# Decay exponents of a state-space mixer from DMA-broadcast rows and a minimum, in place of bfloat16 products on TensorE

## The chip, the cores and the metric

The kernel runs on one core of a Trainium2 chip. The metric is the device time of one execution in microseconds, as the median of several runs; one more execution was profiled. "ScalarE", "VectorE", "GpSimd" and "TensorE" stand as ACT, DVE, POOL and PE in the profile; PEld is TensorE's loading of weights, SP the engine that issues most loads.

## The reference

One layer of a trunk on 128 context tokens and 512 latent tokens, in five tiles of 128 tokens (`NJ` = 5): an input projection, a convolution, a Mamba-2 mixer with 16 heads in both directions beside a pooling mixer, an output projection and a mixture of 16 experts. The change concerns the part of the mixer inside one chunk of 128 tokens:

```python
A_cum = jnp.cumsum(A, axis=-1)                      # A = dt * a, per head
scores = jnp.einsum("bclhn,bcshn->bhcls", Cc, Bc) * jnp.exp(segsum(A))
y_diag = jnp.einsum("bhcls,bcshp->bclhp", scores, xd)   # xd = x * dt
...
y_f, s_f = ssd_direction(..., dt_bias[0], a_log[0], ..., reverse=False)
y_b, s_b = ssd_direction(..., dt_bias[1], a_log[1], ..., reverse=True)
y = (y_f + y_b).reshape(b, L, D_SSD)
y = rmsnorm(y * jax.nn.silu(z.astype(F32)), ssd_norm_w)
```

`exp(segsum(A))` is, for a source token s and a target token t, the exponential of the difference of two cumulative sums, below the diagonal for the forward direction and above it for the backward one.

## The kernel before

Each engine has its program written out by hand in one block; the engines wait for each other by semaphores, and each executes its own program strictly in order. The program runs through these stages: loads and the first norm, the feature projection in 20 tiles (f = 0 to 19, TensorE, L503), the convolution, the products of B and C (`gT`), the pooling products, the chunk states, then the **decay stage**, the output projection (L711), the router and the experts (L815, L827).

The decay stage goes through 40 steps i, two heads of one token tile in each; `j = i // 8` is the token tile. Four steps are a group, numbered g here (`jg` in the code): half the heads of a tile. In step i:

- TensorE, `exponents(i)` (L647 to L665): seven bfloat16 products build the exponents of both heads and both directions in one bank, 512 columns: one with a mask of large negative numbers (L652), two that subtract the cumulative sum of the source token (L656), four that add that of the target token (L662). The sums stand as three bfloat16 pieces each in `tabT`, made by VectorE in L1320 to L1337 from ten products on TensorE (L586).
- ScalarE, `exps(i)` (L958): the exponential, from the bank to a buffer `wbuf`.
- GpSimd (L1167): times dt.
- VectorE, `decay_scores(i)` (L1371, L1374): times `gT`, and forward plus backward.
- TensorE, `diagonal(i)` (L677): the two heads' products with x, from `wbuf`.

Around it stands the gate z of each group, z(g): `project_z(g)`, eight products over k (L575) in one bank, spread over the first three steps of the group before as three, three and two k; ScalarE's `tanh_z(g)` (L951) and VectorE's `silu_z(g)` (L1379), which on their engines stand ahead of the fourth step's work; and the outputs of a group: `from_states` (TensorE, L687, first step, from the second token tile on), `begin_outputs` (VectorE, L1388 to L1396, fourth step, five operations from the second token tile on, one before), `end_outputs` (L1406, L1408, third step of the next group), `turn_y` (TensorE, L697) and `copy_y` (VectorE, L1417). In the last four steps parts of the output projection stand in place of z. On TensorE the diagonal runs three steps behind the exponents:

```python
            for i in range(NS + 3):
                if i < NS:
                    exponents(i)
                    if i % 4 < 3 and i // 4 + 1 < 2 * NJ:
                        project_z(i // 4 + 1, (range(0, 3), range(3, 6), range(6, 8))[i % 4])
...
                if i >= 3:
                    k = i - 3
                    diagonal(k)
```

Of the kernel before, what the change touches and what calls it, by code (L numbers as in the profile page):

```python
# [29 lines left out]
P = 128  # L30
D = 1024
# [19 lines left out]
WBUFS = 6  # L51
# [10 lines left out]
B_STRICT, B_MASK, B_STACK, B_ALL = 0, 128, 384, 416  # L62
# [23 lines left out]
def trunk_kernel(nc, consts, bconsts, vecs, rows, inv, fnorm, x, states0, w_ring, w_late, b_late, w_dt,  # L86
                 w_pool, w_router, w_exp, y_out, s_out):
    ctx = ExitStack()
    with ctx:
# [3 lines left out]
        def sem(name):  # L93
# [5 lines left out]
        slot_out = nc.dram_tensor("slot_out", [SLOTS - P, D], F32).ap()  # L99

# [18 lines left out]
        idb = sb("idb", [P, P], BF16)  # L119
        maskb = sb("maskb", [P, 2, P], BF16)  # L120
        strictb = sb("strictb", [P, P], BF16)
        onesb = sb("onesb", [P, P], BF16)
        stackb = sb("stackb", [96, 32], BF16)
        nstackb = sb("nstackb", [96, 32], BF16)
# [42 lines left out]
        bcst = uf[:, 2 * D:2 * D + B_ALL]  # L167
        tabT = [bf_[0:96, d * 320:(d + 1) * 320].bitcast(BF16) for d in range(2)]
        yt = [bf_[:, 640:1152], ex[:, 11776:12288]]

        wbufs = [ex[:, 8192 + i * 512:8192 + (i + 1) * 512].rearrange("p (h d t) -> p h d t", h=2, d=2)
                 for i in range(WBUFS)]
        sout = [zf[:, 2048 + d * D:2048 + (d + 1) * D] for d in range(2)]
        split_r = [ex[0:32, 8192 + i * TOK:8192 + (i + 1) * TOK] for i in range(2)]
        mid = zf[0:32, 4096:4416].bitcast(BF16)
# [7 lines left out]
        MASK4 = maskb[:, :, :].unsqueeze(1).to_broadcast([P, 2, 2, P])  # L183

        def wbuf(i):
            return wbufs[i % WBUFS]

# [14 lines left out]
        s_bconst = sem("bfloat16_constants_loaded")  # L202
# [52 lines left out]
        s_tabs = sem("decay_tables_split")  # L255
# [7 lines left out]
        s_wd = sem("decays_times_dt")  # L263
        s_e = sem("exponents_built")
        s_ex = sem("decays_exponentiated")
        s_w = sem("scores_decayed")
# [90 lines left out]
        def _(sp):  # L357
# [18 lines left out]
            sp.dma_start(bcst, bconsts).then_inc(s_bconst, 16)  # L376
# [26 lines left out]
            for j in range(NJ):  # L403
                if j == NJ - 1:
# [4 lines left out]
                    sp.wait_ge(s_ex, NJ * HG)  # L409
# [30 lines left out]
        def _(pe):  # L440
# [21 lines left out]
            def ada_late(q):  # L462

                if q == 0:
                    pe.wait_ge(s_dif, 1)
                if q >= 2:
                    pe.wait_ge(s_adr, q - 1)
# [57 lines left out]
            for f in range(20):  # L525
# [25 lines left out]
                if f == 2:  # L551
# [13 lines left out]
            def project_z(jg, ks):  # L565
# [6 lines left out]
                if ks[0] == 0 and jg >= 1:  # L572
                    pe.wait_ge(s_zs, jg)
# [73 lines left out]
            def exponents(i):  # L647
                j, hh = i // HG, 2 * (i % HG)
                o = psb[4 + i % 2]
                if i >= 2:  # L650
                    pe.wait_ge(s_ex, i - 1)
# [1106 lines left out]
```

## Time and profile before

| | |
|---|---|
| median of 3 runs | 1046.53 us (1046.01 to 1047.34) |
| profiled execution | 1048.91 us, span 1047.1 us |
| TensorE busy | 934.5 us, 89% of the span |
| VectorE, GpSimd, ScalarE busy | 360.0, 217.9, 168.9 us |
| decay stage | about 299 to 448 us |
| busy in 380 to 400 us | TensorE 19.60, VectorE 18.59, GpSimd 6.12, ScalarE 4.80 us |
| chain that ended last | TensorE 60%, VectorE 10% |

The profile's busy time of TensorE counts the modelled length of pipelined products, so how long one piece of its work holds up the next is read from start to start in the timeline, not from durations. TensorE's clock is given as the granted share of 2.4 GHz, 1.00 or 0.50.

### The profile page before, as it was taken

Reading aid. Unit: us, or ns where it says so; the run is one execution under the profiler, and the core shown is the slowest. Engines: PE = TensorE matmul, PEld = TensorE weight load, DVE = VectorE, ACT = ScalarE, POOL = GpSimd, SP = SyncE. Lnnn points to the kernel's source line nnn. Section 1 sums busy time; section 2 is a strip of 40 time slices with the busy share of each in tenths; the row PEclk is TensorE's granted clock in tenths of the full one; section 3 lists DMA queues with packets and bytes.
Section 4 is the critical chain, followed back from the end, with each engine's and each line's share of the span. In section 5 each row is a group of like instructions: output and inputs, shape, how many; then the busy total and the mean of one; then the engine's idle time right before and its main releaser. Section 6 shows DMA issues by size and latency. Waiting matters only on the chain.

```text
span 1047.1 us, 13807 instructions
## 1 busy us (share of the span) xinstructions
PE 934.5 (89%) x5470; PEld 631.0 (60%) x5470; DVE 360.0 (34%) x620; ACT 168.9 (16%) x350; POOL 217.9 (21%) x256
## 2 busy tenths in 40 slices
PE   2899999998999999999999449999999999999910
PEld 2565655555545555544444348887888877888800
DVE  2330016446755998733225431110111111111128
ACT  5111012112322222200001200010101111000123
POOL 0189996001422333200000000000000000000053
PEclk9989999999999999999999659999999999999965
DMA  8914657323100002840000418989999999999552
GB/s 356 416 81 161 243 216 285 123 81 121 41 1 1 1 1 81 356 189 20 21 20 21 160 41 305 340 327 333 330 326 351 331 327 333 320 347 326 193 215 106
DMA packets 34451, 205.32 MB, mean 196 GB/s; under 512 B 3760, under 2 KB 6384, under 8 KB 16496
## 3 DMA queue, kind: packets, MB, share of 16 engines
q1 hardware_dynamic: 22896, 169.08, 43.7%
q0 software_dynamic: 5472, 20.45, 5.2%
q10 hardware_dynamic: 6048, 15.30, 3.7%
q8 instruction: 24, 0.39, 0.1%
q14 instruction: 11, 0.09, 0.0%
HBM read 184.86 MB, written 19.96 MB: 196 GB/s over the span
## 4 chain that ended last, share of the span: by engine, by line
PE 60%; DVE 10%; issue 2%; DMA 1%; POOL 1%; ACT 1%; ACTq 0%; POOLq 0%; DVEq 0%
PE bank L815 23%; PE bank L711 13%; PE bank L827 11%; PE bank L575 6%; PE bank L800 2%; DVE ex L1355 1%; PE bank L613 1%; DVE xs L1408 1%; DVE ex L1632 1%; PE bank L764 1%; POOL ex L1167 1%; DVE ex L1371 1%; PE bank L677 1%; DVE uT L1649 1%; DMA ex<-slot_out,ri 1%
## 5 line engine op out<-in xcount | busy, mean ns | idle before, releaser
L815 PEld LDWEIGHTS bank<-yT,ex 128*128 128x128 f32 x2176 | 247.0, 193 | 9.0 <-issue 9.0
L815 PE MATMUL bank<-yT,ex 128*128 128x128 f32 x2176 | 247.2, 276 | 1.0 <-DVE yT L1610 1.0
L503 PE MATMUL bank<-hT,ring 128*128 128x512 f32 (+1 forms) x640 | 179.9, 440 | 2.4 <-DMA ring<-w_ring 2.4
L503 PEld LDWEIGHTS bank<-hT,ring 128*128 128x128 f32 x640 | 96.6, 194 | 73.7 <-issue 70.8
L827 PE MATMUL bank<-ex,yT 128*128 128x512 f32 x272 | 120.9, 597 | 0.0
L1617 DVE TENSOR_TENSOR yT<-yT,bank 128x128 f32<-128x128 f32 x68 | 19.6, 288 | 222.8 <-ACT yT L1029 222.8
L827 PEld LDWEIGHTS bank<-ex,yT 128*128 128x128 f32 x272 | 50.3, 190 | 57.8 <-issue 56.9
L575 PE MATMUL bank<-ring,hT 128*128 128x512 f32 x160 | 76.8, 615 | 4.5 <-DVE ex L1379 2.2
L1176 POOL DMA_INDIRECT yT<-h_dram,idx x17 | 17.3, 1017 | 261.7 <-PE bank L800 261.7
L711 PE MATMUL bank<-ring,yT 128*128 128x512 f32 x160 | 70.2, 593 | 0.8 <-DVE yT L1417 0.8
L1167 POOL TENSOR_TENSOR ex<-ex,dts 128x512 f32<-128x512 f32 x40 | 44.3, 1106 | 101.5 <-ACT ex L958 101.4
L1029 ACT ACTIVATE yT<-bank 128x128 f32<-128x128 f32 x68 | 18.8, 277 | 220.0 <-PE bank L815 220.0
L711 PEld LDWEIGHTS bank<-ring,yT 128*128 128x128 f32 x160 | 30.3, 190 | 38.8 <-issue 37.8
L1621 DVE COPY yT<-bank 128x512 f32<-128x512 f32 x17 | 11.8, 692 | 108.0 <-PE bank L827 108.0
L575 PEld LDWEIGHTS bank<-ring,hT 128*128 128x128 f32 x160 | 28.8, 194 | 32.5 <-issue 26.9
L1371 DVE TENSOR_TENSOR ex<-ex,gT 128x512 f32<-128x512 f32 x40 | 31.9, 797 | 25.9 <-POOL ex L1167 25.9
L1176 POOL DMA_INDIRECT yT<-h_dram,token_of x1 | 1.1, 1098 | 181.5 <-DVE token_of L1601 181.5
L958 ACT ACTIVATE ex<-bank 128x512 f32<-128x512 f32 x40 | 23.9, 597 | 85.1 <-PE bank L662 85.0
L711 PE MATMUL bank<-ring,uT 128*128 128x512 f32 x80 | 36.1, 597 | 0.0
L711 PE MATMUL bank<-hT,uT 128*128 128x512 f32 x80 | 35.3, 594 | 0.8 <-DVE bcT L1396 0.8
L1151 POOL TENSOR_TENSOR ex<-xs,dts 128x1024 f32<-128x1024 f32 x8 | 15.1, 1900 | 97.7 <-DVE xs L1296 80.1
L1308 DVE SCALAR_TENSOR_TENSOR ex<-ex,vec 128x643 f32<-128x643 f32 x36 | 33.8, 939 | 1.3
(260 smaller groups left out, 955.2 us busy)
## 6 DMA issues: line engine op xcount, KB each, us to landing
ex<-w_exp SPq DMA_DIRECT2D x102, 1024.0 KB, 6.7
ring<-w_ring SPq DMA_DIRECT2D x13, 2048.0 KB, 12.3
yT<-w_late SPq DMA_DIRECT2D x16, 1024.0 KB, 6.4
slot_out<-yT ACTq DMA_DIRECT2D x17, 512.0 KB, 8.7
slot_out<-ex POOLq DMA_DIRECT2D x9, 512.0 KB, 12.9
ex<-x SPq DMA_DIRECT2D x5, 512.0 KB, 7.7
xs<-x SPq DMA_DIRECT2D x5, 512.0 KB, 13.5
y_out<-uT SPq DMA_DIRECT2D x5, 512.0 KB, 2.6
```

Of the source, the lines that this page charges most:

```text
L503: mm = pe.matmul(o, w[:, k, (f % 4) * P:(f % 4 + 1) * P], hT[:, k, lo:hi], start=(k == 0), stop=(k == KT - 1))
L575: mm = pe.matmul(psb[6][:, :], hT[:, k, j * P:(j + 1) * P], w[:, k, :], start=(k == 0), stop=(k == KT - 1), skip_group_check=True)
L711: mm = pe.matmul(out_bank(j, hf_, c)[:, :], (yT, uT)[c][:, k, j * P:(j + 1) * P], w[:, k, :], start=(k == 0), stop=(k == KT - 1), skip_gro ...
L800: mm = pe.transpose(psb[2 + k // 4][:, (k % 4) * P:(k % 4 + 1) * P], xg[:, k * P:(k + 1) * P], ident)
L815: mm = pe.matmul(psb[c % 2][:, a * P:(a + 1) * P], w[:, a, k, :], xgT[:, k, :], start=(k == 0), stop=(k == KT - 1))
L827: mm = pe.matmul(psb[6 + hf_][:, :], aT[:, 2 * c + k, :], w[:, k, hf_ * 512:(hf_ + 1) * 512], start=(c == 0 and k == 0), stop=(c == 1 and ...
L958: act.activation(wbuf(i)[:, :, :, :], psb[4 + i % 2][:, :].rearrange("p (h d t) -> p h d t", h=2, d=2), ACT.Exp).then_inc(s_ex, 1)
L1029: act.activation(sg[c % 2], psb[c % 2][:, 0:P], ACT.Silu).then_inc(s_sg, 1)
L1167: pool.tensor_tensor(wbuf(i)[:, :, :, :], wbuf(i)[:, :, :, :], dt_h.unsqueeze(3).to_broadcast([P, 2, 2, P]), ALU.mult).then_inc(s_wd, 1)
L1308: ins = stt(cacc[f % 2], xpad[f % 2][:, q:q + 643], wq, cacc[f % 2], ALU.mult, ALU.add)
L1371: step(tt(w.rearrange("p h d t -> p (h d) t"), w.rearrange("p h d t -> p (h d) t"), gT[:, j, hh // HG, :].unsqueeze(1).to_broadcast([P, 4, ...
L1617: tt(aT[:, c, :], sg[c % 2], psb[c % 2][:, P:2 * P], ALU.mult).then_inc(s_ac, 1)
```

## The change

The cumulative sums of both directions are still made by ten products on TensorE, but early, behind the decay rates in feature tile f = 2. ScalarE copies them on chip and stores them to DRAM by four DMAs, ordered by pair of heads. In the decay stage, ScalarE's queue loads for each step one row of 512 sums (two heads, two directions, 128 target tokens), broadcast to all 128 partitions, into one of three buffers. The exponent comes from one formula for both directions, the minimum of the forward and the backward one, so no mask is needed:

- VectorE, `exponents(i)`: for each head, row of the backward sums plus a number per partition, minimum with the row of the forward sums.
- ScalarE, `exps(i)`: for each head, the exponential with a bias per partition; ahead of it the load of the row of step i + 3.
- ScalarE `mask_forward` and VectorE `mask_both`: for each head, the lower triangle times the forward dt plus the upper triangle times the backward dt, into a buffer `kbuf`.
- GpSimd, `masked_scores(i)`: `kbuf` times `gT`; then `wbuf` times `kbuf`.
- TensorE: `exponents` is gone; `diagonal(i)` stands in step i. z alternates between two banks, so that z(g+1) no longer waits for silu_z(g).

`wbuf` has four buffers of 256 columns in place of six of 512. The bfloat16 constants and their load go.

```diff
@@ project_features, f == 2 (TensorE)
+                    for j in range(NJ):
+                        for d, tri in ((0, trif), (1, trib)):
+                            o = psb[1][64:96, d * P:(d + 1) * P] if j == 0 else \
+                                psb[1][32 * d:32 * d + 32, (j - 1) * P:j * P]
+                            mm = pe.matmul(o, a_[:, j * 32:(j + 1) * 32], tri, start=True, stop=True)
+                    mm.then_inc(s_tab, 1)
@@ project_z
-                if ks[0] == 0 and jg >= 1:
-                    pe.wait_ge(s_zs, jg)
+                if ks[0] == 0 and jg >= 2:
+                    pe.wait_ge(s_zs, jg - 1)
@@ decay stage, TensorE
-            for i in range(NS + 3):
-                if i < NS:
-                    exponents(i)
-                    if i % 4 < 3 and i // 4 + 1 < 2 * NJ:
-                        project_z(i // 4 + 1, (range(0, 3), range(3, 6), range(6, 8))[i % 4])
...
-                if i >= 3:
-                    k = i - 3
-                    diagonal(k)
...
+            for i in range(NS):
+                if i % 4 < 3 and i // 4 + 1 < 2 * NJ:
+                    project_z(i // 4 + 1, (range(0, 3), range(3, 6), range(6, 8))[i % 4])
...
+                diagonal(i)
+                if i % 4 == 0 and i >= 8:
+                    from_states(i // 4)
+                if i % 4 == 1 and i >= 4:
+                    turn_y(i // 4 - 1)
@@ feature tile f == 3, ScalarE
+                    act.wait_ge(s_tab, 1)
+                    act.activation(tabr[0:64, :], psb[1][0:64, :], ACT.Copy)
+                    act.activation(tabr[64:96, 0:256], psb[1][64:96, 0:256], ACT.Copy).then_inc(s_tabc, 1)
...
@@ decay stage, ScalarE
+            def mask_forward(i):
+                j, hh = pair(i)
+                if i >= WBUFS:
+                    act.wait_ge(s_w, i - WBUFS + 1)
+                for q in range(2):
+                    c = j * 32 + hh + q
+                    ins = act.activation(kbuf(i)[:, q, :], trif, ACT.Copy, scale=dt_[:, c:c + 1])
+                ins.then_inc(s_k1, 1)
...
+                act.wait_ge(s_min, i + 1)
+                if i + RBUFS < NJ * HG:
+                    load_rows(i + RBUFS)
+                for q in range(2):
+                    c = j * 32 + hh + q
+                    ins = act.activation(wbuf(i)[:, q, :], wbuf(i)[:, q, :], ACT.Exp, bias=ncum[:, c:c + 1])
+                ins.then_inc(s_ex, 1)
...
                 exps(i)
+                if i + 2 < NJ * HG:
+                    mask_forward(i + 2)
@@ decay stage, GpSimd
+            masked_scores(0)
             for i in range(NJ * HG):
...
+                if i + 1 < NJ * HG:
+                    masked_scores(i + 1)
+                pool.wait_ge(s_kg, i + 1)
                 pool.wait_ge(s_ex, i + 1)
...
+                pool.tensor_tensor(wbuf(i), wbuf(i), kbuf(i), ALU.mult).then_inc(s_w, 1)
@@ decay stage, VectorE
+                dve.wait_ge(s_r[i % RBUFS], 16 * (i // RBUFS + 1))
+                if i >= WBUFS:
+                    dve.wait_ge(s_dg, i - WBUFS + 1)
+                r = rbufs[i % RBUFS]
+                for q in range(2):
+                    ins = stt(wbuf(i)[:, q, :], r[:, q, 1, :], fms[:, j, hh + q:hh + q + 1], r[:, q, 0, :],
+                              ALU.add, ALU.min)
+                ins.then_inc(s_min, 1)
...
                 if i % 4 == 3 and i // 4 + 1 < 2 * NJ:
                     silu_z(i // 4 + 1)
-                decay_scores(i)
+                exponents(i)
+                if i + 1 < NJ * HG:
+                    mask_both(i + 1)
```

On TensorE the order in the second half of one group (z of the next group, then the first step of that group) was, in the kernel before (L575 is z, L677 the diagonal, L652 to L662 the exponents, L687 from_states):

```order
L575 MATMUL bank6<-ring,hT 128x512 x2
L677 MATMUL bank0<-xs,ex 128x64 x2
L652 MATMUL bank5<-maskb,idb 128x512
L656 MATMUL bank5<-nstackb,bcT 128x2x128 x2
L662 MATMUL bank5<-bcT,stackb 128x128 x4
L677 MATMUL bank1<-xs,ex 128x64 x2
L652 MATMUL bank4<-maskb,idb 128x512
L656 MATMUL bank4<-nstackb,bcT 128x2x128 x2
L662 MATMUL bank4<-bcT,stackb 128x128 x4
L575 MATMUL bank6<-ring,hT 128x512 x3
```

In the changed kernel the same place reads as follows (L591 is z, L664 the diagonal, L674 from_states, L684 turn_y):

```order
L591 MATMUL bank4<-ring,hT 128x512 x2
L664 MATMUL bank0<-xs,ex 128x64 x4
L591 MATMUL bank6<-ring,hT 128x512 x3
L664 MATMUL bank1<-xs,ex 128x64 x2
L674 MATMUL bank2<-ex,bcT 128x512
L674 MATMUL bank3<-ex,bcT 128x512
L591 MATMUL bank6<-ring,hT 128x512 x3
L664 MATMUL bank1<-xs,ex 128x64 x2
L684 MATMUL bank7<-cst,xs 128x128 x4
L591 MATMUL bank6<-ring,hT 128x512 x2
```

The diagonals of the third and the fourth step, four products, now stand together directly behind the last two k of z, and the fourth is no longer two exponents and more away from it.

On VectorE the fourth step of a group now reads as follows (L1393 is silu_z, L1386 exponents, L1374 mask_both, L1402 to L1410 begin_outputs); the names in brackets are the semaphores waited for:

```order
L1393 SCALAR_TENSOR_TENSOR btok<-btok,bank6 128x512 [waits tanh_of_half_z,ssd_outputs_combined]
L1386 SCALAR_TENSOR_TENSOR ex<-bcT,dts 128x128 [waits diagonal_products,decay_rows_2_loaded]
L1386 SCALAR_TENSOR_TENSOR ex<-bcT,dts 128x128
L1374 SCALAR_TENSOR_TENSOR ex<-cst,dts,ex 128x128 [waits forward_dt_masked]
L1374 SCALAR_TENSOR_TENSOR ex<-cst,dts,ex 128x128
L1402 TENSOR_TENSOR bcT<-xs,dsum 128x512
L1408 TENSOR_TENSOR ex<-bank2,dts 128x512 [waits state_outputs,dve_steps]
L1410 TENSOR_TENSOR bcT<-bcT,ex 128x512 [waits dve_steps]
L1408 TENSOR_TENSOR ex<-bank3,dts 128x512 [waits dve_steps]
L1410 TENSOR_TENSOR bcT<-bcT,ex 128x512 [waits dve_steps]
L1386 SCALAR_TENSOR_TENSOR ex<-ex,dts 128x128 [waits diagonal_products,decay_rows_0_loaded]
```

Where decay_scores (L1371, L1374 of the kernel before) stood between silu_z and begin_outputs, the start of the step's chain stands now.

## Rows read from the trace of the kernel before

**Rows 1.** Timeline of TensorE, one group: start us, us, engine, line, operation, tiles, count.

```profile
340.29 2.84 PE L575 MATMUL bank<-ring,hT 128*128 128x512 f32 x6 [0.20 <-DVE btok L1379]
342.97 0.55 PE L677 MATMUL bank<-xs,ex 128*128 128x64 f32 x4
343.36 0.61 PE L697 MATMUL bank<-cst,xs 128*128 128x128 f32 x4
343.81 0.38 PE L652 MATMUL bank<-maskb,idb 128*128 128x512 bf16 x1
...
344.47 2.79 PE L575 MATMUL bank<-ring,hT 128*128 128x512 f32 x6
...
351.42 1.94 PE L687 MATMUL bank<-ex,bcT 128*128 128x512 f32 x4
353.19 0.38 PE L652 MATMUL bank<-maskb,idb 128*128 128x512 bf16 x1
...
354.21 1.13 PE L575 MATMUL bank<-ring,hT 128*128 128x512 f32 x2 [0.20 <-DVE btok L1379]
```

**Rows 2.** Timeline of TensorE at the start and the end of the decay stage.

```profile
299.18 0.38 PE L652 MATMUL bank<-maskb,idb 128*128 128x512 bf16 x1
...
447.62 3.70 PE L711 MATMUL bank<-ring,yT 128*128 128x512 f32 x8 [0.78 <-DVE yT L1417]
```

**Rows 3.** Timeline of ScalarE and VectorE behind z(0), whose last product was issued before 299.18.

```profile
299.38 0.60 ACT L951 ACTIVATE btok<-bank 128x512 f32<-128x512 f32 x1 [10.15 <-PE bank L575]
299.99 1.28 ACT L958 ACT_TABLE_LOAD   x1
...
300.08 0.69 DVE L1379 SCALAR_TENSOR_TENSOR btok<-btok,bank 128x512 f32<-128x512 f32 x1 [5.35 <-ACT btok L951]
```

**Rows 4.** Timeline of VectorE, two copies without a wait between them.

```profile
249.78 0.28 DVE L1295 COPY xs<-bank 128x128 f32<-128x128 f32 x1
249.99 0.68 DVE L1296 COPY xs<-bank 128x512 f32<-128x512 f32 x1
```

**Rows 5.** Groups by line and form: count, busy us, mean ns, idle before.

```profile
L1543 DVE SCALAR_TENSOR_TENSOR bcT<-bank,stat,bcT 128x512 f32<-128x512 f32 x10 | 7.5, 751 | 0.4
L1119 POOL TENSOR_TENSOR ex<-ex 128x256 f32<-128x256 f32 x2 | 1.5, 731 | 0.2
```

**Rows 6.** Timeline of ScalarE: two operations without a wait, and a DMA issue.

```profile
262.15 0.37 ACT L929 ACTIVATE uT<-bank,vec 128x128 f32<-128x128 f32 x1 [5.52 <-PE bank L613]
262.42 0.68 ACT L930 ACTIVATE uT<-bank,vec 128x512 f32<-128x512 f32 x1
...
646.85 0.36 ACTq L1035 DMA_DIRECT2D slot_out<-yT  x1
```

**Rows 7.** Timeline of GpSimd and VectorE in one group.

```profile
340.80 1.05 POOL L1167 TENSOR_TENSOR ex<-ex,dts 128x512 f32<-128x512 f32 x1 [1.83 <-ACT ex L958]
340.88 1.25 DVE L1374 TENSOR_TENSOR ex<-ex 128x256 f32<-128x256 f32 x1
342.05 0.68 DVE L1388 TENSOR_TENSOR bcT<-xs,dsum 128x512 f32<-128x512 f32 x1
...
344.94 0.69 DVE L1396 TENSOR_TENSOR bcT<-bcT,ex 128x512 f32<-128x512 f32 x1
...
348.18 0.42 DVE L1374 TENSOR_TENSOR ex<-ex 128x256 f32<-128x256 f32 x1
```

**Rows 8.** Timeline of TensorE: three k of z behind a wait.

```profile
324.75 4.46 PE L575 MATMUL bank<-ring,hT 128*128 128x512 f32 x6 [1.97 <-DVE ex L1379]
```

**Rows 9.** Windows: length, busy PE, PEld, DVE, ACT, POOL, granted clock, DMA share, GB/s.

```profile
326.00:328.00 2.00, 2.00 (x3) 0.78 (x3) 1.52 (x3) 0.00 (x0) 0.00 (x0) 0.50 0.00 0
```

**Rows 10.** Timeline of TensorE: the products of the sums.

```profile
246.66 2.37 PE L586 MATMUL bank<-cst,dts 128*32 128x128 f32 x20
```

**Rows 11.** DMA issues: count, KB each, median us from issue to landing.

```profile
ex<-states ACTq DMA_DIRECT2D x2, 512.0 KB, 4.0
xs<-x SPq DMA_DIRECT2D x5, 512.0 KB, 13.5
```

More of the change, by code:

```diff
@@ L182, in trunk_kernel, with pair, kbuf, z_bank @@
         zero_f = ex[:, 3900:3900 + D]
[L183 removed]
+        def pair(i):
+            return i // HG, 2 * (i % HG)
         def wbuf(i):
             return wbufs[i % WBUFS]
+        def kbuf(i):
+            return kbufs[i % WBUFS]
+        def z_bank(jg):
+            return psb[6 - 2 * (jg % 2)]
         def out_bank(j, hf_, c):
@@ L254, in trunk_kernel @@
         s_tab = sem("decay_tables_summed")
-        s_tabs = sem("decay_tables_split")
+        s_tabc = sem("decay_tables_on_chip")
+        s_tabst = sem("decay_tables_stored")
+        s_fms = sem("forward_less_backward_sums_ready")
+        s_r = [sem(f"decay_rows_{i}_loaded") for i in range(RBUFS)]
         s_g = sem("bc_products")
@@ L581, in _ @@
             pe.wait_ge(s_pad, CONVF)
-            for d, tri in ((0, trif), (1, trib)):
-                q = 2 + 2 * d
-                for j in range(NJ):
-                    o = psb[q + 1][0:32, 0:P] if j == 0 else psb[q][0:32, (j - 1) * P:j * P]
-                    mm = pe.matmul(o, a_[:, j * 32:(j + 1) * 32], tri, start=True, stop=True)
-                mm.then_inc(s_tab, 1)
             for j in range(NJ):
@@ L930, in scale_pooled, with load_rows @@
                 act.activation(uT[:, i, CTX:TOK], lat_in, ACT.Copy, scale=scale).then_inc(s_u, 1)
+            def load_rows(i):
+                j, hh = pair(i)
+                act.dma_start(rbufs[i % RBUFS].rearrange("p h d t -> p (h d t)"),
+                              sums_dram[j, hh // 2].rearrange("h d t -> (h d t)").unsqueeze(0).to_broadcast([P, 4 * P])).then_inc(
+                    s_r[i % RBUFS], 16)
+            for i in range(RBUFS):
+                load_rows(i)
             for i in range(4):
@@ L966, in square_y @@
                                accum_out=stat[:, 16 + jg:17 + jg]).then_inc(s_ys, 1)
+            for i in range(2):
+                mask_forward(i)
             tanh_z(0)
@@ L1418, in copy_y @@
                    vec[:, V_SN + k:V_SN + k + 4].unsqueeze(2).to_broadcast([P, 4, P]), ALU.mult).then_inc(s_yT, 1)
+            mask_both(0)
             silu_z(0)
@@ L1729, in layout @@
     return {
-        "consts": cst, "bconsts": bc, "vecs": vec, "rows": row, "inv": inv,
+        "consts": cst, "vecs": vec, "rows": row, "inv": inv,
         "w_late": w_late, "b_late": b_late.reshape(P, (NQ + 2) * P),
```

163 lines of the change are left out of this document (60 added, 103 removed).

## Prediction

> **What bounds the kernel now.** I read the chain that ended last first. Between 299 and 448 us, the stage that the change rewrites, it runs over TensorE's z products (L575) again and again, with short pieces of GpSimd, VectorE and ScalarE between. The timeline of TensorE for one group of four steps shows why [rows 1]: the group starts at 340.29 and the next at 354.21, so it takes 13.92 us, and the only waits are the two of 0.20 us at the starts. From start to start, three k of z take 2.68 us, a diagonal pair 0.39, turn_y 0.45, one step's exponents 0.66, from_states 1.77; two k of z are as long as from_states. TensorE is the bound here, and the next stages wait for it. So whatever leaves TensorE counts, if nothing else puts a wait in its place. The stage lasts from 299.18, where the last product of z(0) has been issued, to 447.62, where the output projection starts to run without a break [rows 2]: 148.4 us.
>
> **What the change removes.** 40 steps of exponents on TensorE, 40 x 0.66 = 26.4 us. The splitting of the sums on VectorE (L1320 to L1337) lies beside TensorE's pooling products and is done when they are: nothing. VectorE's two products for each step (512 and 256 wide) go, and four 128-wide operations come; ScalarE's 512-wide exponential becomes four 128-wide operations and a DMA issue; GpSimd's one 512-wide product becomes two 256-wide. None of these sums up to the length of a group, so totals don't decide. The order does.
>
> **What the change moves.** In the kernel before, diagonal(i) stands three steps behind exponents(i) on TensorE. In the changed kernel it stands in step i itself, behind the z products of that step. Take group g, and let T be the moment when TensorE has issued the last product of z(g), in step 4g-2. Ahead of it TensorE then has diagonal(4g-2) and directly diagonal(4g-1). But the exponents of step 4g-1 stand on VectorE behind silu_z(g), which waits for tanh_z(g), which waits for z(g). So between T and diagonal(4g-1) lies a chain through four engines, covered by 0.39 us of TensorE's work. The same chain was there before, but with three steps of other products on TensorE under it.
>
> **The chain, from T.** Tanh starts 0.20 after TensorE has gone on, takes 0.60, and silu starts 0.10 later [rows 3]: 0.90. Silu takes 0.69; an operation that waits for nothing starts some 0.08 before the end of the one ahead (a 128-wide copy of 0.28 is followed after 0.21 [rows 4]): exponents begin at 1.51. A VectorE operation with a scalar from a column is some 0.06 longer (751 ns [rows 5] against silu's 0.69), so a pair of 128-wide ones takes 0.27 + 0.34 = 0.61: 2.12. The trace has no such operation in this shape; bounds are 0.49 (no addition) and 0.8. ScalarE then issues the row load (0.36 [rows 6]) and computes two exponentials (0.27 + 0.37 [rows 6]): with hops of 0.03, 3.15. GpSimd has masked_scores(4g) ahead of the product: a 256-wide product with two real streams takes 0.73 [rows 5], and I take that; half of the 512-wide one with a broadcast [rows 7], 0.53, is the bound below. Could masked_scores start when mask_both(4g) is done (2.65), the product would end at 4.14. But the two engines exclude each other: the 256-wide VectorE sum took 0.42 alone and 1.25 when GpSimd's 1.05 us product had started 0.08 earlier [rows 7]. VectorE's begin_outputs starts at 2.55 with a product of 0.68 on two on-chip inputs and holds GpSimd to 3.23. So masked_scores ends at 3.96, the product at 4.70, and TensorE goes on at **4.72**, after 4.3 us of idleness.
>
> **The second chain.** VectorE's begin_outputs has five operations, 0.72 apart [rows 7]. The third meets the product on GpSimd and ends at 5.25, the fifth at 6.69. Only then come exponents(4g) (to 7.22), ScalarE (to 8.25) and GpSimd, with masked_scores(4g+1) ahead (to 9.27): diagonal(4g) can start at **9.30**. TensorE's own way there: 4.72 + 0.39 + 2.68 = 7.8, so it would wait another 1.5 us. After an idleness of 1.97 us, though, three k of z took 4.46 us [rows 8], with the granted clock at 0.50, that is 1.2 of 2.4 GHz, in 326 to 328 [rows 9]. That is 1.6 to 1.8 us more; with 1.6 TensorE is ready at 9.4. The Trainium skill (TensorE: Matmul & The Clock Gate, HAM oscillation) describes loops like this, in which TensorE waits once in every tile and starts each tile at the low clock. By that rule every group pays; the trace agrees in the one place where it has such a gap. Without the loss of clock a full group costs 0.1 us less, since the second chain then sets the end, and only the first two intervals lose the whole.
>
> **The sum.** A full group is 9.40 + 0.39 (diagonal 4g) + 1.77 (from_states) + 2.68 + 0.39 + 0.45 (turn_y) + 1.77 (two k) = **16.85 us** against 13.92. There are seven (T of z(2) to T of z(9)): 118.0. The first interval has a table load of 1.28 [rows 3] in its chain, so that diagonal(0) starts at 5.2: with 0.39 + 2.68 + 1.6 + 0.39 + 1.77, 12.0. The second has no from_states and a begin_outputs of one operation, so no second chain: 4.72 + 0.39 + 2.68 + 1.6 + 0.39 + 2.68 + 0.39 + 0.45 + 1.77 = 15.1. Behind the last T come 9.30, from_states 1.77, four diagonals (1.6), three parts of the projection at 1.77, turn_y 0.45, the eight remaining k (7.1), turn_y and copy_y (1.2): 26.7. Together 171.8 against 148.4: +23.4.
>
> The 10 products of the sums move from 246.66, where they took 2.3 us [rows 10] while TensorE would have waited for VectorE's conversions anyway (copies to 250.67 [rows 4]), to tile f = 2, where TensorE goes from tile to tile and everything behind waits for it. So +2.3; nothing is the bound below. ScalarE's copies and four DMA issues there lie in the time in which it waits for TensorE's next tile: nothing, and 3 us if that cover were gone. The constants' load that is dropped starts nothing earlier that TensorE waits for: nothing.
>
> The sum is +25.7 us. On the profiled execution's own 1048.9 us that makes 1074.6; the median of the runs shown is 1046.5, 2.4 us lower, and the prediction is made for a median: **1072 us**, a ratio of 1.025.
>
> **Row loads.** Each brings 256 KB and is issued three steps ahead. The shortest lead is that of step 4g+2, from 2.15 to some 11 after T: 8.7 us. A 512 KB load by ScalarE's queue took 4.0 us [rows 11], and the DMA share is 0.00 where I looked inside the stage [rows 9]. Only at its end, beside the output weights, did loads need 13.5 us [rows 11]. I take nothing; the bound above is the third rival.
>
> **Rivals.** (1) *Shorter chains*: no loss to the exclusion, none of clock, GpSimd's products at 0.53 to 0.73. Then the second chain ends at 8.3 to 8.8 and a full group takes 15.7 to 16.2; with shorter first intervals (10.4 and 12.9) and the sums' move at nothing to 2.3, +10 to +16: 1056 to 1063. For it: the exclusion is seen at only a few places. (2) *The other side, faster*: VectorE gets to exponents(4g-1) early enough that TensorE never waits. This holds if the chain of 4.72 shrinks to the 0.39 that covers it, or the z products end a step earlier than I read. Then 26.4 us go and 2.3 come: 1022. Against it: each link stands in order behind the one before. An idleness of 2.7 us in each of nine groups would just take up the 24.1 us, and leave 1046. (3) *Late rows*: with 13.5 us a load, the last six to eight steps wait some 2 to 4 us each: +12 to +20 on top, 1084 to 1092. The Trainium skill (DMA: Bandwidth & Descriptors, Issuing engines are not separate DMA queues) says that loads from different engines share the same 16 DMA engines; that speaks for this rival, but by the trace it touches the end of the stage alone. (4) *More exclusion*: two 256-wide GpSimd products and four VectorE operations in each step collide more often than I count. One more collision of 0.73 in each chain gives 18.3 a group, +10: 1082.
>
> **How the numbers follow.** Forecast 0.60, rival 1 0.15, rival 2 0.08, a chain that just cancels 0.03, rival 3 0.06, rival 4 0.08. The likeliest gives 1072; its own range is 1064 to 1080. The 8-in-10 range takes in rivals 1 and 4: 1055 to 1083. A measurement of this kernel tells some 0.2% from no change. Faster 0.08, same 0.03, slower 0.89.
>
> **What would show it.** In the profile after: TensorE idle for about 4 us once in each group, ended by GpSimd's product with diagonal as the waiter; the first z products behind it at the low clock; a group of about 16.9 us; TensorE's busy share of the stage near 70%; VectorE's exponents starting right behind silu and behind begin_outputs. No idle time ended by a row load. The feature stage some 2.3 us later at its end. If TensorE's groups take 11 us (7.1 of z, 1.6, 0.45, 1.77), I am wrong in the order; if they take 14 to 16, in the prices of the chain.

## The result and the profile after

The changed kernel takes 1077.3 us (median of 4 runs, 1073.5 to 1081.0) where the kernel before takes 1046.9 (4 runs, 1046.0 to 1047.7): a ratio of 1.029, 95% interval 1.0245 to 1.0335. It is slower by 30 us; forecast were 1072 us in a range of 1055 to 1083. The profiled execution took 1079.9 us, with a span of 1078.0 us and a mean granted clock of 0.928.

The rows that answer to [rows 1] are one group of four steps on TensorE in the changed kernel (start us, us, engine, line, operation, tiles, count, idle time before and its releaser). T, the moment when the last product of z is issued, is 380.85; the next T is 398.28.

```profile
380.85 0.55 PE L664 MATMUL bank<-xs,ex 128*128 128x64 f32 x4
385.41 1.11 PE L664 MATMUL bank<-xs,ex 128*128 128x64 f32 x4 [4.01 <-POOL ex L1189]
386.32 4.84 PE L591 MATMUL bank<-ring,hT 128*128 128x512 f32 x6
390.99 0.55 PE L664 MATMUL bank<-xs,ex 128*128 128x64 f32 x4
391.38 1.94 PE L674 MATMUL bank<-ex,bcT 128*128 128x512 f32 x4
393.16 2.74 PE L591 MATMUL bank<-ring,hT 128*128 128x512 f32 x6
...
398.28 0.33 PE L664 MATMUL bank<-xs,ex 128*128 128x64 f32 x2
```

TensorE issues diagonal(4g-2) at T and then stands idle for 4.01 us, until GpSimd's product (L1189) releases diagonal(4g-1). The group has lost all of the exponents (the bfloat16 products of [rows 1] are gone) and is still 17.43 us long, where [rows 1] shows 13.92. The other three engines in the same group, first VectorE:

```profile
381.75 0.69 DVE L1393 SCALAR_TENSOR_TENSOR ex<-ex,bank 128x512 f32<-128x512 f32 x1 [4.45 <-ACT ex L954]
382.36 0.61 DVE L1386 SCALAR_TENSOR_TENSOR ex<-ex,dts 128x128 f32<-128x128 f32 x2
382.88 0.61 DVE L1374 SCALAR_TENSOR_TENSOR ex<-cst,dts,ex 128x128 f32<-128x128 f32 x2
383.40 0.69 DVE L1402 TENSOR_TENSOR bcT<-xs,dsum 128x512 f32<-128x512 f32 x1
...
387.28 0.61 DVE L1386 SCALAR_TENSOR_TENSOR ex<-bcT,dts 128x128 f32<-128x128 f32 x2
```

and GpSimd:

```profile
383.57 1.11 POOL L1180 TENSOR_TENSOR ex<-ex,gT 128x256 f32<-128x256 f32 x1 [5.69 <-DVE ex L1374]
384.64 0.72 POOL L1189 TENSOR_TENSOR ex<-ex 128x256 f32<-128x256 f32 x1
388.49 0.77 POOL L1180 TENSOR_TENSOR ex<-ex,gT 128x256 f32<-128x256 f32 x1 [3.13 <-DVE ex L1374]
389.21 0.77 POOL L1189 TENSOR_TENSOR ex<-ex 128x256 f32<-128x256 f32 x1
```

Both chains are there. VectorE stands idle for 4.45 us, until tanh is there, and starts silu (L1393) at T + 0.90; exponents (L1386) follow at 1.51, and GpSimd's product ends at 4.51. The next exponents stand behind begin_outputs (L1402 and four more), at T + 6.43, and their product ends on GpSimd at T + 9.13.

All of these waits in one row, from the groups by line (count, busy us, mean ns, idle before and what ended it), beside the row of the z products:

```profile
L591 PE MATMUL bank<-ring,hT 128*128 128x512 f32 x160 | 91.4, 717 | 0.5 <-DVE ex L1362 0.5
L664 PE MATMUL bank<-xs,ex 128*128 128x64 f32 x160 | 26.8, 296 | 38.3 <-POOL ex L1189 38.0
```

TensorE waits 38.0 us for the diagonals' input in the stage. The stage ends at 478.88, against 447.62 in [rows 2], 31.3 us later.

### The profile page after: what moved, and what is told of

The parts are those of the page before. It is cut to its first block, busy times and chain, and to the rows that moved or that the text cites. A ratio compares the mean times of both kernels' runs of the same rounds, so it can differ in the third digit from the quotient of the medians.

```text
span 1078.0 us, 13542 instructions
## 1 busy us (share of the span) xinstructions
PE 930.1 (86%) x5190; PEld 620.3 (58%) x5190; DVE 348.6 (32%) x677; ACT 195.9 (18%) x472; POOL 235.3 (22%) x292
## 4 chain that ended last, share of the span: by engine, by line
PE 81%; DVE 9%; DMA 3%; issue 3%; ACT 2%; POOL 1%; SPq 0%; DVEq 0%; POOLq 0%; ACTq 0%
PE bank L798 23%; PE bank L513 16%; PE bank L698 12%; PE bank L810 11%; PE bank L591 8%; PE bank L454 2%; PE bank L783 2%; PE bank L664 1%; PE bank L674 1%; DVE ex L1359 1%; PE bank L621 1%; DMA ex<-decay_sums_by_pair 1%; DVE ex L1649 1%; DMA ex<-x 1%; PE bank L747 1%
## 5 line engine op out<-in xcount | busy, mean ns | idle before, releaser
L591 PE MATMUL bank<-ring,hT 128*128 128x512 f32 x160 | 91.4, 717 | 0.5 <-DVE ex L1362 0.5
L664 PEld LDWEIGHTS bank<-xs,ex 128*128 128x128 f32 x160 | 26.2, 216 | 59.4 <-POOL ex L1189 45.6
L664 PE MATMUL bank<-xs,ex 128*128 128x64 f32 x160 | 26.8, 296 | 38.3 <-POOL ex L1189 38.0
L591 PEld LDWEIGHTS bank<-ring,hT 128*128 128x128 f32 x160 | 34.9, 230 | 38.6 <-issue 37.3
L1180 POOL TENSOR_TENSOR ex<-ex,gT 128x256 f32<-128x256 f32 x40 | 33.0, 825 | 110.6 <-DVE ex L1374 110.6
L972 ACT ACTIVATE ex<-ex,dts 128x128 f32<-128x128 f32 x80 | 27.6, 392 | 60.1 <-DVE ex L1386 59.8
L1163 POOL TENSOR_TENSOR ex<-xs,dts 128x1024 f32<-128x1024 f32 x8 | 15.1, 1900 | 99.4 <-DVE xs L1319 81.0
```

The source lines that it names most:

```text
L591: mm = pe.matmul(z_bank(jg)[:, :], hT[:, k, j * P:(j + 1) * P], w[:, k, :], start=(k == 0), stop=(k == KT - 1), skip_group_check=True)
L664: mm = pe.matmul(psb[jg % 2][:, (h % HG) * HD:(h % HG + 1) * HD], wbuf(i)[:, q, :], xs[:, j, h * HD:(h + 1) * HD], start=True, stop=True)
L972: ins = act.activation(wbuf(i)[:, q, :], wbuf(i)[:, q, :], ACT.Exp, bias=ncum[:, c:c + 1])
L1180: pool.tensor_tensor(kbuf(i), kbuf(i), gT[:, j, hh // HG, :].unsqueeze(1).to_broadcast([P, 2, P]), ALU.mult).then_inc(s_kg, 1)
```

## The experiments

Times are medians of 4 to 10 runs, ratios are to the kernel before on the same chip. T(g) is the T of z(g), and "group" the time from one T to the next in the steady part of the stage, from T(3) on. The stage's end is where the output projection starts to run without a break, as in [rows 2].

| kernel | time us | ratio, 95% interval | group us | stage's end |
|---|---|---|---|---|
| changed kernel | 1077.3 | 1.029, 1.0245 to 1.0335 | 16.7 and 17.4 | 478.9 |
| silu behind the step | 1063.0 | 1.0165, 1.0144 to 1.0187 | 16.8 | 460.6 |
| silu and tanh two steps later | 1043.2 | 0.9973, 0.9961 to 0.9986 | 13.6 | 440.5 |
| diagonals two steps late | 1034.1 | 0.988, 0.9853 to 0.9907 | 12.6 | 434.9 |
| rows loaded once | 1075.2 | 1.0264, 1.0231 to 1.0297 | 16.7 and 17.3 | 475.7 |
| stall filled | 1069.8 | 1.0216, 1.0183 to 1.0248 | 16.6 | 466.2 |
| both, two steps each | 1041.4 | 0.9946, 0.9927 to 0.9965 | 13.6 | 439.4 |
| silu two, tanh one step later | 1034.7 | 0.9871, 0.985 to 0.9893 | 12.4 | 436.3 |
| that, and diagonals two late | 1032.6 | 0.9863, 0.9842 to 0.9883 | 12.4 | 430.7 |

**Silu behind the exponents of its own step.** The smallest step out of the first chain, on VectorE, and the same on ScalarE:

```diff
-                if i % 4 == 3 and i // 4 + 1 < 2 * NJ:
-                    silu_z(i // 4 + 1)
                 exponents(i)
                 if i + 1 < NJ * HG:
                     mask_both(i + 1)
+                if i % 4 == 3 and i // 4 + 1 < 2 * NJ:
+                    silu_z(i // 4 + 1)
```

> Edit: in the fourth step of each group, tanh and silu of the next z go behind that step's exponents and exps instead of ahead of them; nothing else moves. Theory (diagonal(4g-1) waits only because its exponents stand behind silu of z(g) in VectorE's queue): the 4 us of idle time of TensorE ahead of diagonal(4g-1) vanish, but exponents(4g) now stand behind silu and begin_outputs, both of which start only 0.9 us after T: silu to 1.6, begin_outputs to 5.2, exponents 5.8, exps 6.9, GpSimd 7.9, while TensorE is through with diagonal(4g-1) and three k of z at 2.4. So one wait of about 5.5 us ahead of diagonal(4g) takes the place of the one of 4 us, and a group takes 7.9 + 7.0 = 14.9 us where the changed kernel takes 17.1: nine groups give 20 us, 1057 us (1052 to 1063). Rival A (only the wait ahead of diagonal(4g-1) counts, and the second chain is not a bound): 38 us come back, 1039. Rival B (the prices of the 128-wide operations and the exclusion of GpSimd by VectorE hold the group, not the order): within 5 us of 1077. Rival C (late row loads): 1077.

It took 1063.0 us. TensorE in one group, with T at 381.62:

```profile
372.53 0.66 PE L664 MATMUL bank<-xs,ex 128*128 128x64 f32 x4 [4.07 <-POOL ex L1189]
373.02 3.12 PE L674 MATMUL bank<-ex,bcT 128*128 128x512 f32 x4
375.93 3.30 PE L591 MATMUL bank<-ring,hT 128*128 128x512 f32 x6
...
381.62 1.00 PE L664 MATMUL bank<-xs,ex 128*128 128x64 f32 x8
382.46 2.79 PE L591 MATMUL bank<-ring,hT 128*128 128x512 f32 x6
389.33 1.11 PE L664 MATMUL bank<-xs,ex 128*128 128x64 f32 x4 [4.08 <-POOL ex L1189]
```

The wait ahead of diagonal(4g-1) is gone: eight records, two diagonal pairs, stand together at T. In its place the next diagonal waits 4.08 us, at T + 7.71; 7.9 was expected. So the second chain is real, and the first one alone (rival A, 1039) is not the whole. My 14.9 for the group was too low: it took 16.80, since behind the wait the clock is low (0.66 from 372.53 to 375.93), from_states takes 2.91 from start to start in place of 1.78 and three k of z 3.14 in place of 2.57. The median lies in the range by that theory (1052 to 1063), at its very end, and this is luck: the steady groups, in which most of the 20 us were to be gained, are hardly shorter (16.80 for a mean of 17.05 in the changed kernel). The gain lies in front of them. From T(1) to T(2) it is 10.78 us in place of 14.93, from T(2) to T(3) 12.29 in place of 17.80: there begin_outputs still belongs to the first token tile and has one operation, so that the second chain is short. So without the first chain a group is fast only where the second is short.

**Silu and tanh two steps later.** On VectorE, and on ScalarE for tanh_z in the same way:

```diff
-                if i % 4 == 3 and i // 4 + 1 < 2 * NJ:
-                    silu_z(i // 4 + 1)
                 exponents(i)
                 if i + 1 < NJ * HG:
                     mask_both(i + 1)
+                if i % 4 == 1 and i >= 4:
+                    silu_z(i // 4)
```

> Edit: tanh and silu of z(g) go two steps later, behind exps and exponents of step 4g+1, so that the exponents of three steps behind T stand ahead of them; every operation, its size and the row loads stay. Theory (the order of VectorE's queue against TensorE's): both chains from T are gone, no idle time of TensorE above 0.5 us behind z, and a group takes what VectorE is busy in it, 11.9 us, or what TensorE is at the full clock, 11.3: nine groups of 12.2 in place of 17.1 give 44 us, 1033 us (1026 to 1040), below the kernel before. Rival B (prices and exclusion hold the group): a group stays above 14 us, 1050 or more. Rival C (row loads): with groups this short, a row load of 3 us and more per step becomes late, VectorE waits for rows at each step, and the group stays at 13.5 or more, 1045 or more.

It took 1043.2 us, above the expected range, and the group 13.6 us in place of 12.2. The 4 us waits are gone; what is left over is a wait of the experiment's own making, on VectorE:

```profile
377.67 0.69 DVE L1393 SCALAR_TENSOR_TENSOR btok<-btok,bank 128x512 f32<-128x512 f32 x1 [1.46 <-ACT btok L954]
```

Silu waits 1.46 us for tanh, which I had put on ScalarE behind the exps of the same step. Rival B (a group above 14) is out. Rival C had named a group of 13.5 or more, but what ends VectorE's wait in each group is tanh; a load ends one wait in the whole stage (4.06 us, at 426.19). And the kernel of silu two and tanh one step later, below, is free of it.

**Diagonals two steps late.** VectorE, ScalarE and GpSimd stay as changed; only TensorE's loop moves:

```diff
-            for i in range(NS):
-                if i % 4 < 3 and i // 4 + 1 < 2 * NJ:
+            for i in range(NS + 2):
+                if i < NS and i % 4 < 3 and i // 4 + 1 < 2 * NJ:
...
-                diagonal(i)
+                k = i - 2
+                if k < 0:
+                    continue
+                diagonal(k)
```

> Edit: TensorE issues diagonal(i-2) in step i in place of diagonal(i), with what follows it; VectorE, ScalarE and GpSimd keep their order, silu ahead of the exponents as in the changed kernel. Theory: behind T TensorE now has diagonal(4g-4), from_states, diagonal(4g-3), turn_y, six k of z and diagonal(4g-2), 7.4 us of work at the full clock, before diagonal(4g-1), whose chain ends at 4.6: the wait is gone from the other side, and the group is again VectorE's 11.9 us and small waits: 1035 us (1027 to 1045). If the stall has its cause on VectorE alone (rival B: prices and exclusion, or C: rows), the order of TensorE changes nothing and the time stays within 5 us of 1077.

It took 1034.1 us, where 1035 was expected. TensorE in one group:

```profile
379.99 0.66 PE L684 MATMUL bank<-cst,xs 128*128 128x128 f32 x4 [1.16 <-DVE xs L1425]
380.49 2.74 PE L591 MATMUL bank<-ring,hT 128*128 128x512 f32 x6
383.06 0.55 PE L664 MATMUL bank<-xs,ex 128*128 128x64 f32 x4
...
388.71 0.63 PE L664 MATMUL bank<-xs,ex 128*128 128x64 f32 x4 [0.30 <-POOL ex L1192]
...
392.61 0.66 PE L684 MATMUL bank<-cst,xs 128*128 128x128 f32 x4 [1.10 <-DVE xs L1425]
```

From 379.99 to 392.61 are 12.62 us, with waits of 1.1 and 0.3 us. No operation is added, dropped or resized against the changed kernel, and the queues of the other engines are the same; the loss of 30 us is a gain of 12.6 (1034.1 against 1046.7 of the kernel before on that chip; it is small, but the interval of the ratio lies below 1). So the place of the diagonals on TensorE made the change slower, and B and C (both at 1077 here) are out as its cause.

**Rows loaded once.**

```diff
-                if i + RBUFS < NJ * HG:
-                    load_rows(i + RBUFS)
...
-                dve.wait_ge(s_r[i % RBUFS], 16 * (i // RBUFS + 1))
+                if i < RBUFS:
+                    dve.wait_ge(s_r[i % RBUFS], 16)
```

> Edit: the row loads are issued for the first three pairs only, and all pairs use these three buffers; Exp takes a constant in place of the exponents, so that values stay finite. It leaves out the right rows, and the routing of tokens to experts can differ, so it is read at the end of the stage of pairs, not by its total alone. Theory: groups stay at 16.7 and 17.4 us with 4 us of idle time behind each z, only the two late rows at the end of the stage (2.48 and 2.05 us of VectorE) go: the stage ends 2 to 4 us earlier. Rival C (the row loads, 37 of them on ScalarE's queue, cost the time): the groups become shorter than 15 us and the stage ends 20 us or more earlier.

It took 1075.2 us; the 4.0 us waits stand in every group as before, and the stage, counted from the start of z(0) (294.14; 293.34 in the changed kernel), is 181.5 us long in place of 185.5. So the row loads are worth 4 us at most, not 20, and the stage's start explains a part of these 4 otherwise, as told at the end. One place shows how late rows cost time. In the changed kernel VectorE waits for two loads at the end of the stage:

```profile
461.72 0.61 DVE L1386 SCALAR_TENSOR_TENSOR ex<-bcT,dts 128x128 f32<-128x128 f32 x2 [2.48 <-DMA bcT<-decay_sums_by_pair]
...
466.26 0.61 DVE L1386 SCALAR_TENSOR_TENSOR ex<-ex,dts 128x128 f32<-128x128 f32 x2 [2.05 <-DMA ex<-decay_sums_by_pair]
```

TensorE's two waits behind these steps, for end_outputs and for begin_outputs, are 2.6 us:

```profile
464.27 0.66 PE L684 MATMUL bank<-cst,xs 128*128 128x128 f32 x4 [1.26 <-DVE xs L1422]
...
470.52 7.13 PE L698 MATMUL bank<-hT,uT 128*128 128x512 f32 x16 [1.33 <-DVE bcT L1410]
```

With rows loaded once both are gone, and T(9) to the end is 28.2 us (447.47 to 475.66) in place of 29.7 (449.14 to 478.88); it isn't shorter by the whole 2.6, as its from_states ran at a mean clock of 0.59 and took 3.01 us in place of 1.77. From the start of z(0) to T(1) it is 16.5 us in place of 20.7, told at the end, and the intervals between are 1.7 longer together.

**Stall filled.** Four products that nobody uses go into TensorE's idle time:

```diff
+                if i % 4 == 3 and i // 4 + 1 < 2 * NJ - 1:
+                    for _ in range(4):
+                        pe.matmul(psb[5][:, :], hT[:, 0, 0:P], hT[:, 0, 0:512], start=True, stop=True)
                 diagonal(i)
```

> Edit: in the fourth step of groups 1 to 8 TensorE issues four products of a part of the normalised input with itself (128x128 by 128x512, float32, into a bank that the stage does not use) ahead of diagonal(4g-1), so that it works through some 3.4 of the 4 us of idle time; the work is surplus and its output is not used. Theory (two chains, the clock only adds to the first): diagonal(4g-1) still waits for GpSimd until 4.6 us behind T, the next three k of z run at the full clock (2.6 us in place of 4.7), TensorE is through at 7.6 and then waits for the second chain until 9.1, where the changed kernel reached diagonal(4g) at 10.1: 1 us a group, in every other group 0.7 more, eight groups give 8 to 14 us: 1066 us (1062 to 1070). Rival D (the low clock alone costs the time, the waits are hidden): the group falls to 14, 1050 or less. Rival B (prices of VectorE and GpSimd): 1077.

It took 1069.8 us (1066.3 to 1071.9). T is 370.92:

```profile
375.49 0.66 PE L664 MATMUL bank<-xs,ex 128*128 128x64 f32 x4 [0.53 <-POOL ex L1192]
375.98 2.79 PE L591 MATMUL bank<-ring,hT 128*128 128x512 f32 x6
380.12 0.66 PE L664 MATMUL bank<-xs,ex 128*128 128x64 f32 x4 [1.34 <-POOL ex L1192]
```

```profile
375.49:380.12 4.63, 3.29 (x11) 1.50 (x11) 4.37 (x10) 1.76 (x6) 1.50 (x2) 1.00 0.21 44
```

The second fence is a window in the order of [rows 9]. TensorE runs at the full clock throughout, and diagonal(4g) still cannot start before T + 9.20: the second chain holds it. The group is 16.59 us (370.92 to 387.51), 0.46 less than the mean of 16.68 and 17.43. Rival D (the clock alone) is out. The expected gain of 1 us in every group was too much: only every other group had something to gain (0.82 to 0.87), since in the others TensorE came to diagonal(4g) at T + 9.38. Most of the gain lies in the two intervals ahead of these groups: T(1) to T(2) took 13.24 us in place of 14.93, T(2) to T(3) 15.03 in place of 17.80, as there the second chain is short and only the clock is lost. From T(1) to T(9) it is 127.9 us at a granted clock of 1.00 in place of 135.1 at a mean of 0.85, 7.2 us less, and the medians differ by 7.5.

**Both cures, two steps each.** The edits of the kernel with silu and tanh two steps later and of the one with the diagonals two steps late, together.

> Edit: both cures at once: TensorE issues diagonal(i-2) in step i, and tanh and silu of z(g) stand two steps later on ScalarE and VectorE. Theory: with diagonals two steps late a group took 12.62 us, of which VectorE is busy 11.9 and waits 0.39 for silu's input and 0.20 for ScalarE's masks; with silu two steps later the 0.39 goes, nine groups give 3.5 us: 1030 us (1027 to 1034). Rival: the two cures are the same one, and the group is held by TensorE's own wait for end_outputs ahead of turn_y (1.1 us): within 2 us of the kernel with the diagonals two steps late, 1034. Rival B, exclusion: with silu elsewhere other pairs of operations of VectorE and GpSimd collide, 1036 to 1045.

It took 1041.4 us, 7 more than the diagonals two steps late alone, so my theory of the sum of two cures fell. The profile shows why: silu waits for tanh for 1.46 us, as in the other kernel with tanh behind the exps of its own step, end_outputs stands behind silu, and TensorE waits for end_outputs:

```profile
382.25 1.12 PE L684 MATMUL bank<-cst,xs 128*128 128x128 f32 x4 [2.62 <-DVE xs L1425]
383.16 5.33 PE L591 MATMUL bank<-ring,hT 128*128 128x512 f32 x6
```

The next two kernels put tanh one step earlier than silu.

**Silu two, tanh one step later.** Against the kernel with both two steps later, on ScalarE alone:

```diff
-                if i % 4 == 1 and i >= 4:
+                if i % 4 == 0 and i >= 4:
                     tanh_z(i // 4)
```

> Edit: diagonals as in the changed kernel; silu of z(g) two steps later (behind exponents of step 4g+1), tanh of z(g) only one step later (behind exps and masks of step 4g). With both two steps later, VectorE stood idle for 1.46 us a group for tanh, which stood on ScalarE behind the exps of the same step, and end_outputs and turn_y came late by as much. Theory (that wait is a consequence of where tanh was put): it goes, a group takes VectorE's busy time and small waits, 12.1 to 12.4 in place of 13.59, nine groups give 12 us: 1031 us (1027 to 1036). Rival (the diagonal of the same step is itself too early, so that TensorE waits for GpSimd however silu is placed): the group stays at 13 or more, 1038 to 1043.

It took 1034.7 us, and the group 12.44: the 1.46 us are gone, and the diagonals of the same step are not too early by themselves.

**The same, with the diagonals two steps late** (TensorE's loop as in that kernel).

> Edit: as the kernel with silu two steps and tanh one step later, and TensorE issues diagonal(i-2) in step i. Theory: VectorE alone sets the group, 12.2 us (11.9 busy, 0.2 for ScalarE's masks), below the 12.62 of the diagonals two steps late alone: 1030 us (1027 to 1033). Rival (end_outputs is late for turn_y however VectorE is ordered, and TensorE then waits 1 to 2.6 us a group): 1034 to 1041.

It took 1032.6 us, the lowest of all, 1.4% below the kernel before (0.9863, 0.9842 to 0.9883). Its group is 12.44 us too, above the expected 12.2; VectorE is busy for 12.04 of these 12.44 us and waits for another engine for 0.19 in all that I found; a part of its work is stretched beside GpSimd (a pair of exponents takes 1.08 in place of 0.61):

```profile
368.20 0.61 DVE L1389 SCALAR_TENSOR_TENSOR ex<-ex,dts 128x128 f32<-128x128 f32 x2
...
369.25 1.08 DVE L1389 SCALAR_TENSOR_TENSOR ex<-ex,dts 128x128 f32<-128x128 f32 x2
370.52 0.81 DVE L1377 SCALAR_TENSOR_TENSOR ex<-cst,dts,ex 128x128 f32<-128x128 f32 x2 [0.19 <-ACT ex L965]
```

The interval overlaps those of the other two good orders, so these runs do not rank the three. In all three VectorE still waits for late rows at the end of the stage: 5.92 us in one step of the kernel with silu two and tanh one step later, 1.74 and 2.03 with the diagonals two steps late, and 2.54, 0.87 and 0.27 in the last one. The order of the queues does not cure that.

**Two kernels for the features**, one execution each. The sums' products issued twice, and, in a second kernel, a load put back where the constants stood (TensorE's first tile waits for it together with the dt weights):

```diff
-                    for j in range(NJ):
+                    for j in 2 * list(range(NJ)):
                         for d, tri in ((0, trif), (1, trib)):
                             o = psb[1][64:96, d * P:(d + 1) * P] if j == 0 else \
```

```diff
             sp.dma_start(wdt, w_dt).then_inc(s_wdt, 16)
+            sp.dma_start(uf[:, 2 * D:2 * D + 416], consts[:, 0:416]).then_inc(s_wdt, 16)
...
-                    pe.wait_ge(s_wdt, 16)
+                    pe.wait_ge(s_wdt, 32)
```

> Edit: the ten products of the cumulative sums that the change put between the features are issued twice in a row into the same place. If the term of the prediction is right (they lie open on TensorE: +2.3 us for ten), the features end 1.9 to 2.3 us later than in the changed kernel. If they are half hidden because TensorE is then at its low clock anyway (they took 1.94 us at a granted 0.74 and at 0.50 alike, and the low stretch ends at a time of its own), they end 0.7 to 1.2 us later. If they are wholly hidden: within 0.3 us.

> Edit: a load of 213 KB is put back on SyncE's queue behind the dt weights, where the removed constants stood; it loads the first 416 columns of the other constants, and nobody uses them. If the removed load is what let the first features start earlier (39.62 us before, 38.58 and 38.21 in two kernels without the load), they start at 39.4 to 39.8 again and the whole kernel ends 1.0 to 1.4 us later than the changed one. If the prediction's nothing is right, they start at 38.2 to 38.6.

They took 1075.0 and 1072.9 us. With the sums twice the features end at 245.2, in the changed kernel at 245.5: no later, though 40 records took 2.89 us where 20 took 1.94. The ends of the features differ by 3 us between executions, told below, so one execution of each does not settle a term of 1 or 2 us. With the load back the first features start at 38.43, within the 38.2 to 39.1 of the ten kernels without it, so the load is not what moved them from 39.62, and the prediction's "nothing" stands. Neither of my two theories on these few microseconds (0.7 to 1.2 later; 39.4 to 39.8) is borne out.

## Why the prediction was right, and where its sizes were off

**The mechanism** held in each link. The order of the queues decided, not the totals, and undoing the order from either side (1034.1 by TensorE, 1034.7 by VectorE and ScalarE) turns the loss into a gain, with all operations of the change in place. Rival 2, the faster side, had just this condition: exponents(4g-1) early enough that TensorE never waits. It asked for 1022; with the order mended it is 1033 to 1035, because VectorE then bounds the group at 12.4 to 12.6 us (busy for 12.04 of 12.44 and 11.86 of 12.62), not TensorE at 11.

**The chain, from T**: 4.72 predicted, 4.56 measured (385.41 less 380.85), silu at 0.90 and exponents at 1.51 as predicted. The bounds on the unknown VectorE shape (0.49 and 0.8) closed at 0.61, and the exclusion is there: masked_scores took 1.11 beside VectorE's product of two on-chip inputs and 0.77 in the second chain. The Trainium skill (GPSIMD Engine Reference, Specifications) names such a contention with VectorE's operations on two SBUF inputs; the rows agree.

**The second chain**: 9.30 predicted, its product ended at 9.13, and the filled stall shows diagonal(4g) at 9.20.

**The sum** is where sizes were off. The stage took 178.6 us (from 300.31, 0.20 ahead of tanh's start as in [rows 3], to 478.88) where 171.8 were predicted: the first interval 13.7 for 12.0, the second 14.9 for 15.1, seven full groups 120.2 for 118.0, the tail 29.7 for 26.7. That is 6.8 too little, of which 1.2 come back because the stage began only 1.1 us later, not 2.3; the profiled execution took 5.3 more than the 1074.6 forecast for it. The term behind most of this is the price of the low clock, which the sum has as 1.6 us in each of the first two intervals and 0.1 in each full group: 3.9. The filled stall shows 7.2 for the eight intervals from T(1) on, and the first interval had another 3.1 of it, which other executions did not have, as told at the end. Without the clock's price the measured intervals are 2.6 us shorter together than the sum has them (the seven full groups 114.7 for 117.3), which hid a part of it. One of the seven full groups is not full: from T(2) to T(3) begin_outputs has one operation, so the second chain is short there too, and 2.77 of its 17.80 us are the price of the clock (15.03 with the stall filled). For a steady group the prediction has "with 1.6 TensorE is ready at 9.4". In windows (as [rows 9]) of two neighbouring groups from diagonal(4g-1) on:

```profile
385.41:390.99 5.58, 5.58 (x10) 2.89 (x11) 5.32 (x13) 2.70 (x10) 2.01 (x3) 0.55 0.19 69
...
368.73:374.00 5.27, 5.27 (x15) 2.58 (x15) 5.01 (x12) 2.39 (x9) 1.70 (x3) 0.68 0.20 68
```

In the group of 380.85 the stretch runs at 0.55 of 2.4 GHz: the diagonal pair takes 0.91 and three k 4.67, and TensorE is ready at 10.14. In the group of 364.17 it is 0.68, and TensorE is ready at 9.38, as predicted. From T(3) on groups of 17.4 and 16.7 alternate around the 16.85 of the forecast. In these steady groups the clock was worth 0.46 us on average, by the filled stall, since the second chain ends hardly earlier. The Trainium skill (TensorE: Matmul & The Clock Gate, HAM oscillation) describes a loop in which a wait in every tile makes each tile start at the low clock. These rows agree in part: every group has a stretch at the low clock behind its wait, but in every other group it begins only behind the diagonal pair (granted 1.00 from 368.73 to 369.23, 0.50 from 370 to 373).

**The tail** was short of the late rows. "Row loads: I take nothing" failed in two steps of 40 (2.48 and 2.05 us), a small part of rival 3, whose own figures, six to eight steps at 2 to 4 us, make +12 to +32 and not +12 to +20. TensorE's waits behind these two steps, 1.26 and 1.33 us, are most of the 3.0.

**The sums moved**: +2.3 predicted, not seen. T(0) is 1.1 us later than before (300.31 to 299.18), and the features end 0.5 earlier (245.5 and 246.0). The nearest comparison is of executions with the same granted clock from 70 to 84 us (0.76): from the first feature product to their end it is 206.4 us in the kernel before (39.62 to 245.99), and 207.1 and 207.6 in two kernels with the change (38.21 to 245.29, 38.65 to 246.21), 0.7 to 1.2 more. With a spread of 3 us there, told at the end, that the stage began 1.2 us earlier than predicted is luck. TensorE's busy share of the stage was 77% (136.9 of 178.5 us), not 70%.

Rivals 1, 3 and 4 did not come about: no group of 15.7 to 16.2, no 12 to 20 us of late rows, no 18.3 a group. That the order's two chains would cost nearly the same as the exponents saved (1046) did not come either.

## What to carry to other kernels

When work moves off the bound engine, ask first in which order each engine's queue meets its inputs, and only then what the operations cost: here one operation (silu) ahead of the next exponents in VectorE's queue, with the diagonal that needs them directly behind the products of z on TensorE that silu waits for, turned some 12 us of gain into 30 us of loss. A wait of a strict queue can be taken away on either side, by issuing the consumer later or by putting the late operation behind the urgent ones. When an operation moves to a later place, its producer on the other engine must still stand a step ahead of it: tanh behind the exps of silu's own step cost 8.5 us (1043.2 to 1034.7, on two chips; by the ratios 1.0%).

## What the runs showed of the hardware

- **The clock around diagonal(0).** In the changed kernel ScalarE's table load stands behind a row load and starts 2.25 us after the start of tanh (300.51 to 302.76); with rows loaded once it starts 0.62 after it (301.31 to 301.93). Diagonal(0) waits 2.62 us in the one and 1.46 in the other, and three k of z behind it took 5.23 us from start to start in the one and 2.63 in the other. It looks as if 1.2 us of wait had made 3.8 of time, but the length of the wait doesn't decide it. Five kernels have the same wait of 2.62 us there: in two (the changed kernel, and silu two and tanh one step later) the granted clock behind it was 0.50 and the three k took 5.23 us, in three (silu behind the step, silu and tanh two steps later, stall filled) it was 1.00 and they took 2.63. So the first interval was 13.7 us in the changed kernel and 10.6 in those three, behind the same code; what decides it stays open. The changed kernel, rows loaded once, and silu behind the step:

```profile
305.67 1.12 PE L664 MATMUL bank<-xs,ex 128*128 128x64 f32 x4 [2.62 <-POOL ex L1189]
306.57 5.43 PE L591 MATMUL bank<-ring,hT 128*128 128x512 f32 x6
```

```profile
305.31 0.66 PE L664 MATMUL bank<-xs,ex 128*128 128x64 f32 x4 [1.46 <-POOL ex L1187]
305.80 2.79 PE L591 MATMUL bank<-ring,hT 128*128 128x512 f32 x6
```

```profile
302.86 0.66 PE L664 MATMUL bank<-xs,ex 128*128 128x64 f32 x4 [2.62 <-POOL ex L1189]
303.36 2.79 PE L591 MATMUL bank<-ring,hT 128*128 128x512 f32 x6
```

- **A spread of 3 us ahead of the change's stage.** Ten profiles of kernels with the same code up to there (one with the sums twice among them) end their features between 243.4 and 246.2 us. The granted clock from 70 to 84 us goes with it: 1.00 in the three that end between 243.4 and 243.8, 0.88 in five from 243.9 to 245.5, 0.76 in the two at 245.3 and 246.2. The products of the sums took 1.08 us in the first three and 1.94 in the changed kernel. A term of 2 us there cannot be read from one profile of each kernel; why the clock falls in one execution and not in the next stays open.
